# Part of an FFN's outer projection as Strassen products, and two exchanges in TensorE's order in an attention

## The reference, cut to what matters

```python
def conv_ffn(h, conv_prev, w_in, conv_w, conv_b, w_out):
    u, gate = jnp.split(h @ w_in, 2, axis=-1)
    ext = jnp.concatenate([conv_prev.astype(u.dtype), u], axis=1)
    a = conv_b + sum(ext[:, j:j + T] * conv_w[j] for j in range(CONV_W))
    out = (jax.nn.silu(a) * gate) @ w_out      # (576 x 2816) @ (2816 x 1024): the outer projection
    return out, ext[:, -(CONV_W - 1):]
```

```python
logits = s + (cqi[..., :, None] - cum_k[..., None, :])      # s = q k^T / 8
p = jax.nn.softmax(jnp.where(mask, logits, -jnp.inf), axis=-1)
return jnp.einsum('bhqk,bkhd->bqhd', p.astype(v.dtype), v)
```

## Time and profile before

| | us |
|---|---|
| median of 3 runs (1566.13 to 1567.67) | 1566.71 |
| the profiled execution's own time | 1566.23 |
| its span in the trace | 1564.7 |
| TensorE busy | 1532.6 |
| VectorE busy | 953.8 |
| ScalarE busy | 748.6 |
| GpSimd busy | 459.5 |

### The profile page before, as it was taken

The page is one execution under the profiler, slowest core; times in us unless marked ns, Lnnn a source line. Parts: engine busy times, 40 slices in busy tenths (PEclk is TensorE's granted clock), DMA queues, the critical chain, the costliest instruction groups (busy, mean ns, idle before and its releaser), DMA issues. The chain is left out here.

```text
span 1564.7 us, 36647 instructions
## 1 busy us (share of the span) xinstructions
PE 1532.6 (98%) x13694; PEld 1454.8 (93%) x13694; DVE 953.8 (61%) x1700; ACT 748.6 (48%) x1283; POOL 459.5 (29%) x495
## 2 busy tenths in 40 slices
PE   7999999999999999999999999999999999999997
PEld 7999999989999999999999999655899999999997
DVE  6667666656977676633354444678449867676221
ACT  6444444435466666522344455666444656565110
POOL 1222222214475655010010100222135765551000
PEclk9999999999999999999999999999999999999999
DMA  6222322213233232222333434599422323232330
GB/s 214 69 87 86 91 86 77 77 55 116 68 109 108 80 107 83 78 84 84 94 120 117 129 96 148 195 349 347 145 76 81 108 81 107 81 103 88 97 103 25
DMA packets 52883, 174.14 MB, mean 111 GB/s; under 512 B 7266, under 2 KB 9330, under 8 KB 52770
## 3 DMA queue, kind: packets, MB, share of 16 engines
q1 hardware_dynamic: 47858, 155.46, 30.7%
q0 software_dynamic: 4912, 17.12, 3.0%
HBM read 159.99 MB, written 12.57 MB: 110 GB/s over the span
## 5 line engine op out<-in xcount | busy, mean ns | idle before, releaser
L534 ACT ACTIVATE w_hi<-w_raw 128x1024 fp32r<-128x1024 f32 (+1 forms) x143 | 146.9, 1027 | 302.2 <-PE acc L2046 266.8
L1037 DVE TENSOR_TENSOR w_lo<-w_raw,w_hi 128x1024 fp32r<-128x1024 f32 (+1 forms) x141 | 171.9, 1219 | 144.0 <-ACT w_hi L534 142.3
L2046 PE MATMUL acc<-xl,w_hi 128*128 128x288 f32 x1008 | 227.7, 307 | 7.9 <-DVE xl L1049 7.4
L2046 PE MATMUL acc<-xh,w_hi 128*128 128x288 f32 x1008 | 216.3, 296 | 0.0
L2046 PE MATMUL acc<-xh,w_lo 128*128 128x288 f32 x1008 | 216.1, 296 | 0.0
L2046 PEld LDWEIGHTS acc<-xl,w_hi 128*128 128x128 f32 x1008 | 162.1, 190 | 16.6 <-issue 13.9
L2238 PE MATMUL aux<-ffn_xsh,w_lo 128*128 128x288 f32 x576 | 169.9, 295 | 0.0
L2238 PE MATMUL aux<-ffn_xsh,w_hi 128*128 128x288 f32 x576 | 169.7, 295 | 0.0
L2238 PE MATMUL aux<-ffn_xsl,w_hi 128*128 128x288 f32 x576 | 169.4, 294 | 0.2
L2046 PEld LDWEIGHTS acc<-xh,w_hi 128*128 128x128 f32 x1008 | 162.7, 189 | 0.0
L2046 PEld LDWEIGHTS acc<-xh,w_lo 128*128 128x128 f32 x1008 | 162.4, 189 | 0.0
(11 more groups left out here) (341 smaller groups left out, 3435.3 us busy)
## 6 DMA issues: line engine op xcount, KB each, us to landing
w_raw<-w_fi_in SPq DMA_DIRECT2D x88, 512.0 KB, 3.8
w_raw<-w_fo_in SPq DMA_DIRECT2D x32, 512.0 KB, 3.6
att_Vd<-cache_v_in SPq DMA_DIRECT2D x32, 512.0 KB, 5.6
w_raw<-w_mix_in SPq DMA_DIRECT2D x31, 512.0 KB, 3.7
w_raw<-w_kv_in SPq DMA_DIRECT2D x16, 512.0 KB, 3.7
w_raw<-w_qg_in SPq DMA_DIRECT2D x16, 512.0 KB, 3.6
dec_Kd<-cache_k_in SPq DMA_DIRECT2D x16, 512.0 KB, 6.6
w_raw<-cache_k_in SPq DMA_DIRECT2D x16, 512.0 KB, 7.4
```

The lines of the kernel that those rows point to most:

```text
L534: nc.scalar.activation((w_hi[:, pos.slot % SPL] if dst is None else dst)[:, 0:width], w_raw[:, pos.slot, 0:width] if raw is None else raw[ ...
L1037: nc.vector.tensor_tensor(low[:, 0:width], w_raw[:, pos.slot, 0:width] if raw is None else raw[:], high[:, 0:width].bitcast(F32), ALU.subt ...
L2046: mm = nc.tensor.matmul(dst[:, hf, 0:HALF], W[:, 128 * (j0 + j):128 * (j0 + j) + 128], x[:, HALF * hf:HALF * hf + HALF], start=(first and ...
```

## The change

Of the 22 inner tiles of the outer projection, tiles 8 to 15 (block c = 1) are worked as Strassen-Winograd products for the output tiles in pairs (2, 3), (4, 5) and (6, 7). The 2x2 blocks are: output tiles m0 and m1, inner tiles 8 to 11 and 12 to 15, and the two token halves. Eight block products of 12 matmuls (4 inner tiles x 3 terms) become seven. Blocks c = 0 and c = 2, and output tiles 0 and 1, stay as they were. The token side's four sums for each j of 4 (tiles 8+j and 12+j) are made once in a layer; the weight side's four for each pair. Two intermediate products are read out of a PSUM bank and added to `h` by VectorE (`read_add`). The x parts of layer 0's end are made together in the last pair, since the summed tokens lie in their memory. The loops of two rounds over four output tiles are written out. The blocks are loaded in the new order.

In the attention `score(i, 1)` stands ahead of `pv(i - 1, 2)`, and `sample_turn(i - 1)` ahead of `turns(i, 2)`.

```diff
+FO_ORDER = [(m, c) for m in range(2) for c in range(3)]
+for m in range(2, DT, 2):
+    FO_ORDER += [(m, 1), (m + 1, 1), (m, 0), (m, 2), (m + 1, 0), (m + 1, 2)]
...
 (SP)
+                for n, (m, c) in enumerate(FO_ORDER):
+                    w = 128 * len(FO_K[c])
+                    load(Pos(b_out + n), d[f"w_fo{layer}"][m][:, 1024 * c:1024 * c + w], w,
+                         ready=(lo_done, b_out + n - 2) if n > 6 and n % 6 == 4 else None)
...
 (ScalarE, behind the 22 high parts)
+                def fo_hi_tokens(j):
+                    act.wait_ge(fo_sum, fo_part_n(fo_sum, layer, 1) - 12 + 4 * j)
+                    for q in range(4):
+                        nc.scalar.activation(fo_high(j, q), fo_plain(j, q), ACT.Copy).then_inc(fo_hi, 1)
+                fo_hi_tokens(0)
+                fo_hi_block(3)
+                fo_square(0)
+                fo_hi_block(4)
+                fo_hi_tokens(1)
+                fo_hi_block(5)
+                fo_hi_tokens(2)
+                fo_hi_tokens(3)
+                for p in range(1, DT // 2):
+                    n, got = 6 * p, fo_part_n(fo_sum, layer, p)
+                    fo_hi_block(n)
+                    act.wait_ge(fo_sum, got + 2)
+                    nc.scalar.activation(fo_w[:, 0, 0], aux[:, 1], ACT.Copy).then_inc(fo_hi, 1)
+                    act.wait_ge(fo_sum, got + 3)
+                    nc.scalar.activation(fo_w[:, 1, 0], aux[:, 2], ACT.Copy).then_inc(fo_hi, 1)
+                    fo_square(2 * p - 1)
+                    pos = Pos(b_out + n + 1)
+                    act.wait_ge(block_done, b_out + n)
+                    act.wait_ge(w_in[pos.slot], 16 * pos.lap + 16)
+                    nc.scalar.activation(w_hi[:, 1, 512:1024], w_raw[:, pos.slot, 512:1024], ACT.Copy).then_inc(hi_done, 1)
...
 (VectorE, behind the 22 low parts)
+                def fo_tokens(j):
+                    got = fo_part_n(fo_sum, layer, 1) - 16 + 4 * j
+                    b1, b2 = halves(gx[:, 2 + j]), halves(gx[:, 6 + j])
+                    dve.wait_ge(gh_ok, FT * (layer + 1))
+                    dve.wait_ge(glo_ok, FT * (layer + 1))
+                    t1, t2, t3, t4 = [fo_plain(j, q) for q in range(4)]
...
+                    nc.vector.tensor_tensor(t1, b1[:, 1], b1[:, 0], ALU.subtract).then_inc(fo_sum, 1)
+                    nc.vector.tensor_tensor(t3, b2[:, 1], b1[:, 1], ALU.subtract).then_inc(fo_sum, 1)
+                    dve.wait_ge(fo_sum, got + 1)
+                    nc.vector.tensor_tensor(t2, b2[:, 1], t1, ALU.subtract).then_inc(fo_sum, 1)
+                    dve.wait_ge(fo_sum, got + 3)
+                    nc.vector.tensor_tensor(t4, b2[:, 0], t2, ALU.subtract).then_inc(fo_sum, 1)
+                    for q in range(4):
+                        dve.wait_ge(fo_hi, fo_part_n(fo_hi, layer, 1) - 15 + 4 * j + q)
+                        nc.vector.tensor_tensor(fo_low(j, q), fo_plain(j, q), fo_high(j, q).bitcast(F32), ALU.subtract)\
+                            .then_inc(fo_lo, 1)
...
+                fo_tokens(0)
+                fo_lo_block(3)
+                fo_add(0)
+                fo_lo_block(4)
+                fo_tokens(1)
+                fo_lo_block(5)
+                fo_tokens(2)
+                fo_tokens(3)
+                for p in range(1, DT // 2):
...
+                    fo_lo_block(n)
+                    (sums 1, 2, 3 of r0, r1 into aux[:, 1], aux[:, 2], aux[:, 3]; each waits for the one before)
+                    part_lo(1, fo_w[:, 0, 1], aux[:, 1], fo_w[:, 0, 0])
+                    (sum 4 into aux[:, 1])
+                    part_lo(2, fo_w[:, 1, 1], aux[:, 2], fo_w[:, 1, 0])
+                    if p > 1:
+                        dve.wait_ge(fo_read, read)
+                    fo_add(2 * p - 1)
+                    (low part of the second half of block n + 1)
+                    dve.wait_ge(fo_ps, ps + 1)
+                    read_add(m0, 0, aux[:, 0]).then_inc(fo_read, 1)
+                    part_lo(3, w_lo[:, 1, 0:512], aux[:, 1], w_hi[:, 1, 0:512])
+                    dve.wait_ge(fo_ps, ps + 2)
+                    read_add(m0, 1, c22).then_inc(fo_read, 1)
+                    dve.wait_ge(fo_ps, ps + 3)
+                    dve.wait_ge(fo_read, read + 2)
+                    read_add(m0, 1, aux[:, 0]).then_inc(fo_read, 1)
+                    part_lo(4, fo_w[:, 0, 1], aux[:, 3], fo_w[:, 0, 0])
+                    fo_lo_block(n + 2)
...
 (TensorE)
+                for n in range(6):
+                    fo_block(n, n % 3 == 0, n % 3 == 2)
+                for p in range(1, DT // 2):
...
+                    pe.wait_ge(lo_done, b_out + n + 1)
+                    if p > 1:
+                        pe.wait_ge(fo_read, read)
+                    fo_product(aux[:, 0], w_hi[:, 0, 0:512], w_lo[:, 0, 0:512], fo_raw(8, 0), False).then_inc(fo_ps, 1)
+                    pe.wait_ge(evac, t_out + m0 - 1)
+                    fo_product(c11, w_hi[:, 0, 512:1024], w_lo[:, 0, 512:1024], fo_raw(12, 0), False).then_inc(block_done, 1)
+                    pe.wait_ge(evac, t_out + m1 - 1)
+                    pe.wait_ge(fo_lo, low + 1)
+                    fo_product(c22, fo_w[:, 0, 0], fo_w[:, 0, 1], fo_summed(0), False).then_inc(fo_ps, 1)
+                    pe.wait_ge(fo_lo, low + 2)
+                    pe.wait_ge(fo_read, read + 1)
+                    fo_product(aux[:, 0], fo_w[:, 1, 0], fo_w[:, 1, 1], fo_summed(1), True).then_inc(fo_ps, 1)
...
+                    fo_block(n + 2, False, False)
+                    fo_block(n + 3, False, True)
+                    fo_block(n + 4, False, False)
+                    fo_block(n + 5, False, True)
...
                     sample_scores(i - 1)
+                    score(i, 1)
                     pv(i - 1, 2)
-                    score(i, 1)
                     turns(i, 0)
...
                 pv(i, 1)
-                turns(i, 2)
                 if prev:
                     sample_turn(i - 1)
+                turns(i, 2)
```

More of the change, by code:

```diff
@@ new lines, in ffn @@
+                fo_hi_tokens(0)
[18 more added lines that the diff above has]
+                    nc.scalar.activation(w_hi[:, 1, 512:1024], w_raw[:, pos.slot, 512:1024], ACT.Copy).then_inc(hi_done, 1)
+                    act.wait_ge(fo_sum, got + 4)
+                    nc.scalar.activation(w_hi[:, 1, 0:512], aux[:, 1], ACT.Copy).then_inc(fo_hi, 1)
+                    act.wait_ge(fo_ps, fo_ps_n(layer, p) + 2)
+                    nc.scalar.activation(fo_w[:, 0, 0], aux[:, 3], ACT.Copy).then_inc(fo_hi, 1)
+                    fo_hi_block(n + 2)
+                    fo_hi_block(n + 3)
+                    if g_next is not None and p == DT // 2 - 1:
+                        for m in range(DT - 2):
+                            gain_hi(xh, m, g_next)
+                    fo_hi_block(n + 4)
+                    fo_square(2 * p)
+                    if g_next is not None and p == DT // 2 - 1:
+                        gain_hi(xh, DT - 2, g_next)
+                    fo_hi_block(n + 5)
@@ new lines, in fo_add, with fo_x_lo, read_add @@
+                def fo_add(m):
+                    add_h(m, b_out + max(n for n, at in enumerate(FO_ORDER) if at[0] == m), (t_out + m) % 2, h_base + 8 + m + 1)
+                def fo_x_lo(m):
+                    if g_next is not None:
+                        gain_lo(xl, xh, m, g_next, x_base + 8 + m)
+                def read_add(m, hf, bank):
+                    to = h[:, m, HALF * hf:HALF * hf + HALF]
+                    return nc.vector.tensor_tensor(to, to, bank[:, 0:HALF], ALU.add)
+                fo_tokens(0)
@@ L2281, in ffn, with fo_block @@
                 gate_first(1, FT - 1)
-                with pe.Fori(0, 2) as i:
-                    for m in range(4):
-                        for c, kts in enumerate(FO_K):
-                            gemm(Pos(b_out + 3 * m + c, i, 12), t_out + 4 * i + m, (t_out + m) % 2, kts, goh, gol,
-                                 first=(c == 0), last=(c == 2), wait_x=(glo_ok, FT * layer) if m == 0 else None)
+                def fo_block(n, first, last):
+                    m, c = FO_ORDER[n]
+                    gemm(Pos(b_out + n), t_out + m, (t_out + m) % 2, FO_K[c], goh, gol, first=first, last=last, joins=m > 1,
+                         wait_x=(glo_ok, FT * layer) if m == 0 else None)
@@ new lines, in fo_product @@
+                def fo_product(dst, wh, wl, xs, add):
+                    for j in range(4):
+                        c = slice(P * j, P * j + P)
+                        xh_, xl_ = xs(j)
+                        for n, (W, X) in enumerate(((wh, xl_), (wl, xh_), (wh, xh_))):
+                            mm = nc.tensor.matmul(dst[:, 0:HALF], W[:, c], X, start=(not add and j == 0 and n == 0), stop=(j == 3 and n == 2),
+                                                  skip_group_check=True)
+                    return mm
```

127 lines of the change are left out of this document (92 added, 35 removed).

## The result

The changed kernel takes 1572.42 us (median of 6 runs, 1571.53 to 1573.76), the kernel before 1566.63 us (6 runs): ratio 1.0036, 95% interval 1.0026 to 1.0046. It is slower by 5.8 us, where about none was forecast and 1570.8 was the upper end of the range.

What follows compares the result with a forecast made beforehand. TensorE, busy 98% of the span, was taken as the bound, with the outer projection one unbroken piece. Terms: -9.5 + 5.8 + 4.25 + 1.6 - 2.2 = -0.05, so 1566.6 us on the median's scale; range 1561.5 to 1570.8.

Steps and rivals of the forecast that it cites:

- block 3 late, two layers: Outer projections: token sums queued ahead of block 3's split leave TensorE idle 2.9 us in each layer, 5.8 us.
- pairs, layer 1: Second layer's products: first pair's third product 1.5 us late, its fourth 0.15, later pairs in time; 1.65 us.
- pairs, layer 0: First layer's products: 1.5 us at the first pair's third, 0.7 at its fourth, 0.2 late twice in later pairs; 2.6 us.
- The first pair's third product: Outer projection: it takes over a bank of tile 1, waits for VectorE's addition of that tile, and is 1.5 us late.
- the first exchange: Attention: the score ahead of pv of unit 2 brings what follows 0.32 us earlier; seven rounds, 2.2 us.
- the second exchange: Attention: the 0.2 us sample transpose fills the 0.34 us wait, but brings nothing beyond the score's move ahead of pv.
- Rival 1: Outer projections: sums hide, block 3 only 1.4 late per layer, pairs cost half, clock holds; -6.8, 1559.9 us; chance 0.16.
- rival 3: Attention: its loads bound it and the exchanges bring nothing; 1568.8 us; chance 0.09.
- rival 4: Outer projections: all seven products late by more than their gain, so the saving isn't there; 1576.0 us; chance 0.03.
- I take one fall out of two: Outer projections: TensorE's clock falls to 1.2 GHz behind one of two 2.9 us stalls; 1.6 us, bounds 0 and 3.2.
- rival 2: Outer projections: clock falls to 1.2 GHz behind both long stalls and both of 1.5 us; +4.8, 1571.4 us; chance 0.15.
- six pairs late like the first of layer 0: Outer projections: upper bound of the pairs' cost in both layers together, given as 12 us.

Runs made afterwards that it cites:

- the products alone: The changed kernel with the attention's order as before, so only the Strassen products remain: 1573.58 us, 1.0047 of the kernel before.
- the square later: The changed kernel with ScalarE's square of tile 2p - 1 moved behind the two high parts of block n + 1: 1568.63 us, 1.0010 of the kernel before.
- both exchanges alone: The kernel before with the two exchanges in the attention and no Strassen products: 1565.51 us, 0.9992 of the kernel before.
- the filled wait: The changed kernel with 20 matmuls into a free bank, result unread, ahead of block 3 in each layer: 1570.21 us, 1.0022 of the kernel before.
- the early block 3: The changed kernel with block 3's high and low parts ahead of the first token sums on ScalarE and VectorE: 1567.31 us, 1.0003 of the kernel before.
- the first alone: The kernel before with only pv of unit 2 moved behind the score that follows it in the attention: 1564.64 us, 0.9987 of the kernel before.
- GpSimd later: The changed kernel with GpSimd waiting in layer 0 until VectorE has made the half split: 1571.27 us, 1.0038 of the kernel before.
- all cures: The changed kernel with block 3 split first, the square later, and the first pair's tile 1 added ahead of the weight sums: 1563.11 us, 0.9976 of before.

## Why the prediction was wrong

By its own terms, for the profiled executions:

| term | forecast us | measured us |
|---|---|---|
| matmuls saved | -9.5 | -9.5 (72 fewer) |
| block 3 late, two layers | +5.8 | +6.0 |
| pairs, layer 1 | +1.65 | +1.8 (1.6 + 0.17) |
| pairs, layer 0 | +2.6 | +5.4 (1.6 + 1.7 + 2 x 1.04) |
| clock in the projections | +1.6 | +4.0 (2.6 + 1.4) |
| the attention's rounds | -2.2 | -2.0 (7 x 0.28) |
| the attention's first round | 0 | +1.1 |
| sum | -0.05 | +6.8 (spans: +6.7) |

The clock's share in a projection is what the changed kernel's execution has beyond that of the products alone, whose clock was 1.00: 6.2 - 3.6 and 1.5 - 0.1. In the attention the first round, from the transposes at 998.81 to those at 1015.46, took 16.65 in place of 15.83 (992.52 to 1008.35), although the exchange took 0.28 off it. About 0.95 of the 1.1 are the clock, since the run with the square later has the same order and the same wait of 2.69 us in that round, no fall, and 15.70; the rest goes with that wait, which is 2.69 us in every kernel with three pairs and 2.41 in the others, for a reason that was not looked for.

*Right.* The queue in front of block 3 was forecast to 0.1 us: ScalarE's four copies, then its high part, then VectorE's low part, and 2.9 late. The first pair's third product (1.5, measured 1.6), the fourth of layer 1 (0.15, measured 0.17), the rate of the matmuls and the first exchange (0.32 a round, measured 0.28) hold, and the second exchange brings nothing. The 0.04 that the round gained less lie at the score: with both exchanges alone it starts at 1033.14, 0.05 behind the end of the exponential's row (1032.88 + 0.21), where the prediction had the bank free 0.05 ahead of such a row's end. Rival 1 falls with the row at 1440.78; rival 3 with the rounds; rival 4 with the later pairs, whose third products are on time.

*The step that failed first: the fourth products of layer 0.* The prediction put VectorE's half split at 0.69 and had it 0.7 late in the first pair and 0.2 in the two later ones, counting the square as ScalarE's time alone. The square also releases GpSimd, whose addition of 1.4 us then stands in the way of the half split. By the trace the sum of the term is 5.4, 2.8 more than forecast, and the edit that removes the lateness of the fourth products is worth 4.1 (2.2). The overlap alone is 2.4 of it; with GpSimd held back the three fourth products are late by 0.7, 0.2 and 0.2, as the prediction had them. It could have been seen in the trace of before, where VectorE's operation at 667.46 takes 1.51 us beside GpSimd's addition in place of 0.81; the prediction says only that GpSimd's squares "stay in their order", which is true and not the question. The Trainium skill (SBUF — State Buffer, "Who interferes with whom") states that a VectorE instruction with two inputs in SBUF contends with a GpSimd instruction that reads SBUF, and calls the shared port pair "an exclusive lock". The trace agrees in the main: the half split ends 0.55 and 0.56 us after GpSimd's end, where it takes 0.69 by itself.

*The step that failed second: "I take one fall out of two: 1.6 us".* The two stalls of block 3 brought 6.8 us of low clock in layer 0 and 3.4 in layer 1, which cost 4.0 where 1.6 stood. The attention's stall brought 6.8 us, where the kernel before has 3.4, and cost another 1.0. This was rival 2 in kind, and its figure of 1571.4 lies nearest to the median; but not as it was worked out. That the measured median lies near it is luck: the stalls of 1.3 to 1.4 us never lowered the clock, in no execution, and a stall of 2.7 could bring 6.8 us of low clock, which cost 2.6 in layer 0 and which no case had. How often it falls is not fixed by the kernel: see below. Over the runs the filled wait gives 2.2 us (2.1) for the projections' part, so the forecast's 1.6 was no bad mean, and the profiled execution (1573.28, above the median) has the lowest mean clock of its six, 0.994. Why three of the changed kernel's runs are near 1571.6 and three near 1573.4 stays open: only the profiled execution has its clock by stretches, and the mean clock of the whole span doesn't sort them (0.995, 0.997 and 0.995 against 0.994, 0.996 and 0.996), though 3.4 us of low clock move it by only 0.001.

*Two bounds don't follow from their own terms.* With block 3's high part made early, VectorE's 3.7 us less the 1.5 to spare leave 2.2 late and not 1.4, so that rival 1 would have stood at about 1561.5; and six pairs late like the first of layer 0, 2.2 us each, are 13.2 and not 12. Neither touches the sum of the forecast or the two steps above.

What stays open: by the medians the kernel loses 5.8 us. Taking the clock's falls away gives back 2.2, the fourth products 4.1 and the early block 3 5.2 with the clock's part in it, each within about 2; the finer shares rest on single traces.

## What to carry to other kernels

An engine that is idle more than a third of the time can still be late: before work is given to it, follow its queue at the one place where the work has to be done, and give it out in pieces between the splits that TensorE waits for; two thirds of the products, with the sums spread out and the square later, gained 7.5 us where all of them in a lump lost 5.8. An operation moved beside another engine's has to be priced with what that engine is set off to do, since VectorE's and GpSimd's operations stand in each other's way. Price a stall in a dense stretch from start to start and not by the idle time shown, and give a long one a chance of the low clock on top.

## What the runs showed of the hardware

The clock behind a stall of 2.4 to 2.8 us is a matter of the execution: kernels that run the same instructions up to the stall differ in it. In the attention's first round twelve profiled executions have such a stall (2.41 or 2.69 us): three show no fall (both exchanges alone, the first alone, the square later), four show 3.4 us at 1.2 GHz, five show 6.8 us, and the kernel before is among the four. At block 3 eight such stalls were profiled (the changed kernel, the products alone, GpSimd later, the square later, two each): four without a fall, three with 3.4 us, one with 6.8. In a dense stretch of 288-column matmuls a pair of them takes 0.48 us from start to start at 1.2 GHz and 0.26 at 2.4, so that 3.4 us at the low clock cost 1.5 and 1.6 us where it lay behind the idle time (GpSimd later, the square later), and 1.4 where 0.3 of it lay in the idle time (the changed kernel, layer 1). In the attention's first round 3.4 us of low clock cost nothing that shows: the round takes 15.70 us with it (all cures, GpSimd later) and 15.70 without (the square later), where a wait of 1.05 us stands that the other two don't have. 6.8 us of it cost 0.95 there in the changed kernel and more in others. Behind 1.1 to 2.1 us of idle time by itself, in the projections and the attention, no execution has a fall. A profile of one execution therefore can't price such a stall; several runs of a kernel with the wait filled can.

While GpSimd adds 128x576 elements (1.41 us), VectorE's subtraction of 128x512, both inputs in SBUF, takes 1.42 and 1.50 us in place of 0.69. In the kernel before, beside the same addition (1.43 us), VectorE's scaled subtraction of 128x576 takes 1.51 in place of 0.81.
